# When a tile's eight routing heads run: 7.5 positions apart from 64, parts two positions apart

## What is computed

```python
q = (xb @ w_query).reshape(PEER_BLOCK, PEER_HEADS, 2, half)
s = jnp.einsum('thpc,hpkc->thpk', q, sub_keys)
top_s, top_i = lax.top_k(s, PEER_TOPK)                    # 16 of 128 keys, two sides
cand_s = (top_s[:, :, 0, :, None] + top_s[:, :, 1, None, :]).reshape(...)
cand_e = (top_i[:, :, 0, :, None] * N_KEYS + top_i[:, :, 1, None, :]).reshape(...)
best_s, best_j = lax.top_k(cand_s, PEER_TOPK)             # 16 of 256 pairs
experts = jnp.take_along_axis(cand_e, best_j, axis=-1)
gate = jax.nn.softmax(best_s, axis=-1)
u, vv = jnp.take(expert_u, e_flat, axis=0), jnp.take(expert_v, e_flat, axis=0)
act = jax.nn.gelu(jnp.einsum('td,tkd->tk', xb, u), approximate=False)
coef = (gate * act)
out = jnp.einsum('tk,tkd->td', coef, vv)
```

## Time and profile before

| | before |
|---|---|
| median of 3 runs | 3422.01 us |
| lowest and highest | 3419.47 and 3422.57 us |
| the profiled execution | 3425.16 us |
| its span, first to last instruction | 3423.4 us |
| VectorE, TensorE, ScalarE, GpSimd busy | 79%, 75%, 21%, 37% of the span |
| mean granted TensorE clock | 0.876 |
| DMA | 1386.73 MB, mean 405 GB/s |

### The profile page before, as it was taken

The page is one execution under the profiler, slowest core; times in us unless marked ns, Lnnn a source line. Parts: engine busy times, 40 slices in busy tenths (PEclk is TensorE's granted clock), DMA queues, the critical chain, the costliest instruction groups (busy, mean ns, idle before and its releaser), DMA issues.

```text
span 3423.4 us, 40003 instructions
## 1 busy us (share of the span) xinstructions
PE 2563.8 (75%) x14040; PEld 1166.1 (34%) x14040; DVE 2710.1 (79%) x7309; ACT 715.3 (21%) x1565; POOL 1262.7 (37%) x1092
## 2 busy tenths in 40 slices
PE   6976597677668776767777777876787667789876
PEld 5444345322332233233323332333243323234321
DVE  6388897897898889887988798979897975455865
ACT  2210232033103310331024102420142012121100
POOL 0122223134434444453445443544444332234442
PEclk8998798898889898998888888988899878889999
DMA  9999999999999999999999999999999999999999
GB/s 332 382 398 370 376 385 383 417 419 421 415 406 412 421 415 411 404 420 411 414 403 416 421 416 381 409 418 421 407 409 419 421 411 423 419 416 392 418 398 377
DMA packets 218457, 1386.73 MB, mean 405 GB/s; under 512 B 28424, under 2 KB 39176, under 8 KB 67336
## 3 DMA queue, kind: packets, MB, share of 16 engines
q0 software_dynamic: 156672, 1140.92, 81.2%
q1 hardware_dynamic: 40000, 137.63, 10.5%
q10 hardware_dynamic: 21584, 105.63, 7.8%
HBM read 1370.99 MB, written 80.04 MB: 424 GB/s over the span
## 4 chain that ended last, share of the span: by engine, by line
DVE 39%; DMA 27%; PE 20%; issue 11%; ACT 2%; POOL 1%; ACTq 0%; POOLq 0%; SPq 0%; DVEq 0%
DMA t<-in_expert_uv,t 26%; DVE t L1109 12%; PE psum L1487 10%; DVE t L976 5%; PE psum L1389 3%; DVE psum L1136 3%; PE psum L1430 2%; DVE t L1121 2%; DVE t L1057 2%; DVE t L1055 2%; DVE t L1058 2%; DVE t L1056 1%; PE psum L1311 1%; DVE t L1054 1%; DVE t L1008 1%
## 5 line engine op out<-in xcount | busy, mean ns | idle before, releaser
L648 POOL DMA_INDIRECT t<-in_expert_uv,t x1088 | 1262.5, 1160 | 2126.7 <-PE psum L1483 862.7
L1487 PE MATMUL psum<-t,t 64*64 64x512 f32 x4896 | 1348.3, 689 | 619.6 <-DVE t L1121 618.6
L1109 DVE CUSTOM_DVE_ANT_0 t<-t,t 128x1024 f32<-128x1024 f32 x1088 | 1321.7, 1222 | 468.9 <-DMA t<-in_expert_uv,t 454.5
L1487 PEld LDWEIGHTS psum<-t,t 64*64 64x64 f32 x4896 | 342.9, 149 | 1442.8 <-DVE t L1121 846.4
L1483 PE MATMUL psum<-t,t 64*64 64x512 f32 x2496 | 766.0, 742 | 0.0
L808 ACT ACTIVATE t<-t 128x2 f32<-128x2 f32 x544 | 110.8, 204 | 1842.1 <-DVE t L1109 1810.5
L1430 PEld LDWEIGHTS psum<-t,t 128*128 128x128 f32 x2304 | 278.9, 201 | 72.7 <-issue 66.5
L1430 PE MATMUL psum<-t,t 128*128 128x128 f32 (+1 forms) x2304 | 289.9, 287 | 2.6 <-ACT t L770 2.6
L1311 PE MATMUL psum<-t,t 128*128 128x128 f32 (+2 forms) x768 | 254.6, 492 | 10.4 <-DMA t<-in_xT 6.4
L976 DVE SCALAR_TENSOR_TENSOR t<-t,t,t 128x128 f32<-128x128 f32 x840 | 238.2, 346 | 0.0
L1483 PEld LDWEIGHTS psum<-t,t 64*64 64x64 f32 x2496 | 173.3, 155 | 0.1
(11 more groups left out here) (142 smaller groups left out, 2067.0 us busy)
## 6 DMA issues: line engine op xcount, KB each, us to landing
t<-in_wq_t ACTq DMA_DIRECT2D x65, 1024.0 KB
out<-in_cache_k_win SPq DMA_DIRECT2D x8, 4080.0 KB
out<-in_cache_v_win SPq DMA_DIRECT2D x7, 4080.0 KB
t<-in_w_in_t ACTq DMA_DIRECT2D x44, 512.0 KB, 9.4
t<-in_kc_t SPq DMA_DIRECT2D x8, 2560.0 KB, 17.9
t<-in_vc_t SPq DMA_DIRECT2D x8, 2560.0 KB
t<-in_expert_uv,t POOLq DMA_INDIRECT x1088
t<-in_w_v_t ACTq DMA_DIRECT2D x6, 1024.0 KB
```

The source lines that it names most:

```text
L648: pool.indirect_dma_start(ring[:, r, :], None, I["expert_uv"], bass.IndirectOffsetOnAxis(ap=idn[t % 2][:, s:s + 1], axis=0)).then_inc(land ...
L1109: dve.tensor_tensor_reduce(out=ring[:, r, 0:D], in0=x1[t % 2][:, :], in1=ring[:, r, 0:D], scale=1.0, scalar=0.0, op0=ALU.mult, op1=ALU.add ...
L1487: last = pe.matmul(MAIN[t][half][NS * a:NS * a + NS, :], zt[NS * a:NS * a + NS, k % Z_RING, j, :], vv[NS * a:NS * a + NS, :], start=(c == ...
```

## The change

Head h's routing starts at position 64 + floor(7.5 h): 64, 71, 79, 86, 94, 101, 109, 116 in place of 65, 72, 79, 86, 93, 100, 107, 114. Its parts stand at offsets 0, 2, 4 and 6 in place of 0, 2, 4 and 5. `QUERY_AT` follows: 14, 15, 17, 19, 21, 23, 25, 27 in place of 14, 16, 17, 19, 21, 23, 24, 26, so the queries of head 1 move from position 67 to 63, those of head 6 from 99 to 103, and those of head 7 from 107 to 111, with their key scores and copies. The last experts move from 119 to 122. In step -1 the dots begin at position 71 in place of 72, and the early exponentials stand at 70, 77 and 85 in place of 71, 78 and 85. The sample tile's routing has positions of its own, which stay.

```diff
-ROUTE_AT = 65
-ROUTE_STEP = 7
-QUERY_AT = [(ROUTE_AT + ROUTE_STEP * _h) // 4 - 2 for _h in range(8)]
+ROUTE_AT = [64 + 15 * _h // 2 for _h in range(8)]
+QUERY_AT = [_q // 4 - 2 for _q in ROUTE_AT]
...
-        lo, hi = (min(max(q + j - ROUTE_AT - ROUTE_STEP, 0), EARLY) for j in range(2))
+        lo, hi = (min(max(q + j - ROUTE_AT[1], 0), EARLY) for j in range(2))
...
-                            if n == -1 and 4 * g + i == ROUTE_AT + ROUTE_STEP * (h + 1) - 1:
+                            if n == -1 and 4 * g + i == ROUTE_AT[h] + 6:
                                 gate_exp(0, h + 1, range(h, h + 1))
...
-                h, at_ = divmod(4 * g + i - ROUTE_AT, ROUTE_STEP)
-                if 0 <= h < PH:
+                for h in range(PH):
+                    at_ = 4 * g + i - ROUTE_AT[h]
                     if at_ in (0, 2):
                         route_side(m, h, at_ // 2)
                     if at_ == 4:
                         route_pairs(m, h)
-                    if at_ == 5:
+                    if at_ == 6:
                         route_experts(m, h)
-                if m == 0 and at_ == ROUTE_STEP - 1 and 0 <= h < EARLY_GATES:
-                    gates(0, range(h, h + 1))
-                if m == 0 and at_ == 1 and 1 <= h <= EARLY_GATES:
-                    gates_end(0, h, range(h - 1, h))
+                        if m == 0 and h < EARLY_GATES:
+                            gates(0, range(h, h + 1))
+                    if m == 0 and at_ == 1 and 1 <= h <= EARLY_GATES:
+                        gates_end(0, h, range(h - 1, h))
```

## The result

| | before | after |
|---|---|---|
| median of 14 runs each, side by side | 3422.12 us | 3425.93 us |
| lowest and highest | 3416.91 and 3426.59 us | 3424.26 and 3432.53 us |
| span of the profiled execution | 3423.4 us | 3428.1 us |
| mean granted TensorE clock | 0.876 | 0.875 |

The ratio is 1.0017, with a 95% interval of 1.001 to 1.0025: slower by 3.8 us in the medians and by 3.4 to 8.6 us in the interval, not 21 us faster. The forecast of 3401 and its range both missed. (In the kernel after, every line number is one lower than in the one before.)

The account below looks back on a forecast made before the run. Transfers set the pace in mid-step, but wait for VectorE at steps' ends and from 310 to 360 us. Gains of 14.9 and 6 us, together 20.9, gave 3401 us at the median, range 3384 to 3420.

Parts of the forecast that it names:

- The tails: Last 60 us of routing in six steps: transfers wait for VectorE; the parts' new places win 14.9 of 26.1 us.
- no two parts share such an interval: Between two weighings, with parts at offsets 4 and 6: the longest interval is 6.3 us, against 9.3 before.
- 2.6 us a step: At a step's end VectorE's worst lag behind the transfers falls from 10.4 to 7.8 us, counted as gain per step.
- the sign that the prediction named for being wrong: Time saved at the steps' ends comes back as VectorE waiting for rows later; no size given.
- all burst: At the steps' ends, back-to-back pairs and experts cause the whole loss: 26.1 + 6 us goes, 3390 us; chance 0.14.
- the cited rule: Gathers: fixed 2.0 us plus bytes over 436 GB/s, so two in flight keep engines full and only long gaps starve.
- no change: At the steps' ends transfers are slow, not missing: only 5.5 us won, 3416.5 us; chance 0.16.
- The first step: Before tile 0's full step, VectorE's waits of 3.3 and 8.8 us go: 6 us taken, bounds 0 and 12.1.
- It counts in full: First step's 6 us all shorten the total, as transfers from 310 to 360 us wait for VectorE.
- Move the same bytes: nothing.: SyncE's cache copies behind head 2 of tile 0 and head 6 of tile 1 start later at no cost.
- The sample tile's keys: First sample keys after tile 7's start about 4 us later: 0 taken, 4 us kept for the upper end.
- The slower rival: Score copies of heads 0 and 7 come too late, VectorE waits before the side: 46 us more, 3447 us; chance 0.08.

Follow-up runs that it names:

- experiment 2: Each half of the change alone: kernel before with experts at offset 6, 3424.61 us (1.0006); changed kernel with experts at offset 5, 3427.8 us (1.0022).
- experiment 3: Less VectorE work, a head's row numbers from one addition: on the kernel before 3415.41 us (0.9986), on the changed kernel 3414.97 us.
- experiment 5: Residual two positions earlier: first run, on experiment 3's edit of the kernel before, 3422.95 us; second, on the changed kernel with last cache copy behind head 5's query, 3423.72.
- experiment 6: Kernel before: half the output columns left out for 60 of 64 pairs, 3424.52 us; waits instead, 3423.22; 16 waits a position added on TensorE, 3422.82; on ScalarE, 3449.0.
- experiment 4: First step's cache copies 5 to 8 moved later: kernel before, 3421.29 us (0.9997); changed kernel with last copy behind head 5's query, 3430.6 us (1.0024).

## Why the prediction was wrong

**The tails** (term 14.9). The reading of the tail was right in place, and the size came near: 12.3 us went. For the size that is in part luck, as the reason given, the interval between two weighings, is not borne out (experiment 2). It was also read wrongly: "no two parts share such an interval" is not so, since the experts of heads 0 and 4 (70 and 100) stand between the same two weighings as the next head's first side (71 and 101), and the longest interval is 2.70 + 3.00 + 1.83 = 7.5 us by the prediction's own prices, not 6.3; the trace has 7.8 and 7.5 there. The step that failed is the next one, that a gain of "2.6 us a step" in the tail is 2.6 us of the step. The loss moved to the following positions, and VectorE waited 7.8 us longer for rows in the four steps, which is the sign that the prediction named for being wrong. Experiments 3 and 5 show how firm this is. VectorE was relieved of 72.5 us in four steps, and the two longest intervals were taken apart; the steps stayed within 1389 to 1393 us, and VectorE waited for rows instead (129, then 204 us).

What holds the steps there is open. One thing that the trace shows could do it. A gather reports its landing in 16 parts, and VectorE's dot waits for the last. Taken from the landing records of the kernel before (means over the steps of tiles 1 to 6), the last part lands 2.9 us behind the first for positions 0 to 7 of a step and 6.4 us at 96 to 103. In experiment 5's first run, where no pause stops the transfers for long, it is 7.0 at the start and 7.2 or more from position 88 on. Parts that land early wait with their places held, and the ring has only ten. If the places run out by that, the DMA engines that are ahead stand still for those behind, in a pause or without one, and a pause in the tail, which lets the late parts catch up, costs little. The Trainium skill (DMA: Bandwidth & Descriptors, section Why a DMA increments its semaphore by 16 and not by 1) says that the engines of a transfer finish independently; the trace agrees with these 3 to 8 us. Against the drift as the cause stands a pair of runs: with waits on TensorE's queue (experiment 6) the parts lie 2.6 us apart at the start and 6.4 at 96 to 103, in experiment 5's run 7.0 and 7.9, and the four steps take 1388.5 and 1390.3 us. What makes the parts drift is open too: it is neither TensorE's instruction packets nor the places of the rows, and no edit here took the drift itself away, so this cause is argued and not shown.

**The rival "all burst"** rested on the cited rule, by which only a long gap starves the engines. Experiment 2 speaks against it here: the long waits went from the tails, and the tails stayed as they were.

**The rival "no change"** had its time (3416.5) and its sign (tails as low as before) wrong, but the trace supports its reading of the shortfall as partly slow transfers. In the kernel before, the rate in the first three tails is 8 to 10% below 421 GB/s and the DMA share only 3 to 4% below 1.01. By the packet records an expert row of 8 KB takes a mean of 327 to 332 ns in the first four tails and 314 ns from 1100 to 1160 us. By the share, the six tails won (6.01 - 5.90) x 60 = 6.6 us, not 12.3.

**The first step** (term 6, bounds 0 to 12.1). Both waits went, and the lower bound came true: 13.0 us more of waiting for rows. "It counts in full" failed. The step's end follows VectorE's own work (experiment 3's 11 us), and a wait before that is filled by another (experiment 4).

**"Move the same bytes: nothing."** The copies' start was costed by bytes alone. In the right place the last copy fills a stretch that gathers leave empty; behind head 6's new position it left 8.4 us of transfers undone. Making it later still in the kernel before, behind head 7's query, cost 15.9 us; undoing it after gave back 2.4 to 4.4. The sample tile's keys, held at 0 with 4 us kept for the upper end, started 10.7 us later, and next to no time was lost by it: the steps of tiles 6 and 7 together take 800.4 us, 798.3 before, and 798.2 to 799.1 in the other three traces with the new routing.

**The slower rival** (score copies of heads 0 and 7) did not come about: over the whole span VectorE waits once for a score copy, the 12.2 us above.

## What to carry to other kernels

A stretch where the transfers run below their rate is a loss that can be won only if the whole period, from one step's start to the next, gets shorter; before forecasting, relieve the suspected engine in a trial and see whether its waits for data grow by as much. And a wait that gates a bulk copy is a price, not a number of bytes: ask what else would fill the engines until it starts.

## What was not expected of the hardware

Nearly half of TensorE's value matmuls (3,360 of 7,392) could go without any effect on the time, and its mean granted clock fell with them, from 0.876 to 0.767. Within one kernel the clock also fell behind a short idle time. TensorE's timeline after, at the start of the step for tile 6:

```profile
2463.33 1.98 PE L1330 MATMUL psum<-t,t 64*128 64x512 f32 x4
2465.24 7.41 PE L1486 MATMUL psum<-t,t 64*64 64x512 f32 x32
2474.97 1.97 PE L1341 MATMUL psum<-t,t 128*128 128x128 f32 x8 [2.33 <-ACT t L714]
2476.87 3.78 PE L1330 MATMUL psum<-t,t 64*128 64x512 f32 x4
2480.58 9.31 PE L1486 MATMUL psum<-t,t 64*64 64x512 f32 x32
```

Behind a wait of 2.33 us for ScalarE's exponential the same four matmuls take 3.78 in place of 1.98 us, and 32 values matmuls 9.31 in place of 7.41; the granted clock, a mix of its two levels, is 0.67 behind the wait, where it is 1.00 in the 11.7 us before it:

```profile
2463.00:2474.70 11.70, 9.54 (x38) 2.73 (x36) 9.24 (x22) 2.51 (x3) 6.21 (x6) 1.00 1.01 422
2474.70:2490.00 15.30, 15.03 (x46) 5.60 (x47) 14.23 (x41) 9.71 (x14) 3.19 (x3) 0.67 0.79 313
```
